# Layer 3 of a fused four-layer forward pass: its distance mask moved into a bias table, its k and v made one group

## What is computed

```python
def odd_layer(x, norm_g, w_in, q_gain, k_gain, sinks, w_out, rel_bias):
    h = rms_norm(x, norm_g) @ w_in                # 2048 -> q 2048, k 256, v 256, gate 2048
    q, k, v, gate = split_cols(h, ODD_SPLITS)
    q = rms_norm(q.reshape(B, T, 32, 64), q_gain)
    k = rms_norm(k.reshape(B, T, 4, 64), k_gain)
    o = swa_sink_attention(q, k, v, sinks, rel_bias)
    return x + (jax.nn.silu(gate) * o) @ w_out

# in swa_sink_attention, W = 128; i a query of a block, j a key of this block or the one before
dist = W + i[:, None] - j[None, :]
bias = rel_bias[t5_bucket(dist)]                  # one number per distance and head
in_window = (dist >= 0) & (dist < W)
logits = jnp.where(mask, logits + bias, -jnp.inf) # then softmax with a sink per head, then times v
```

## Time and profile before

| | |
|---|---|
| median of 3 runs | 1672.68 us (1670.34 to 1673.58) |
| the profiled execution, its own time | 1674.83 us |
| its span | 1672.7 us |
| PE busy | 1524.3 us (91%) |
| PE weight load busy | 1337.2 us (80%) |
| DVE busy | 1085.3 us (65%) |
| ACT busy | 696.4 us (42%) |
| POOL busy | 57.0 us (3%) |
| mean DMA rate | 205 GB/s |
| mean granted clock of TensorE | 0.965 of full |

### The profile page before, as it was taken

The page is one execution under the profiler, slowest core; times in us unless marked ns, Lnnn a source line. Parts: engine busy times, 40 slices in busy tenths (PEclk is TensorE's granted clock), DMA queues, the critical chain, the costliest instruction groups (busy, mean ns, idle before and its releaser), DMA issues.

```text
span 1672.7 us, 25093 instructions
## 1 busy us (share of the span) xinstructions
PE 1524.3 (91%) x9839; PEld 1337.2 (80%) x9839; DVE 1085.3 (65%) x1847; ACT 696.4 (42%) x1186; POOL 57.0 (3%) x86
## 2 busy tenths in 40 slices
PE   5888999988949999999959999999997799989998
PEld 0657789987849888998849998889886798879986
DVE  3436677888977635676675476975646757786563
ACT  1324234334335323444335354544544345655442
POOL 3000000000000000000000000000003300000000
PEclk9898999999979999999979999999999999999999
DMA  9997888997837665775646655326664553334572
GB/s 353 380 380 228 260 273 286 346 348 278 321 130 229 208 181 163 240 259 181 191 138 179 182 147 171 112 76 181 184 185 135 162 165 101 114 114 129 176 220 92
DMA packets 184070, 342.94 MB, mean 205 GB/s; under 512 B 28972, under 2 KB 47632, under 8 KB 183184
## 3 DMA queue, kind: packets, MB, share of 16 engines
q1 hardware_dynamic: 179920, 326.88, 60.7%
q0 software_dynamic: 4032, 14.46, 2.5%
HBM read 339.14 MB, written 2.15 MB: 204 GB/s over the span
## 4 chain that ended last, share of the span: by engine, by line
PE 76%; DVE 9%; DMA 5%; ACT 4%; issue 3%; SPq 2%; POOLq 0%; POOL 0%; DVEq 0%; ACTq 0%
PE PM L1345 63%; PE PB L1345 9%; DMA stg<-in_w_in 3%; SPq L1267 2%; ACT AR L1665 2%; ACT whi L1665 2%; DVE X L1887 1%; PE PB L1517 1%; DVE AC L1887 1%; DVE wlo L1962 1%; PE PB L1489 1%; PE PB L1592 1%; DMA AR<-in_w_in 1%; DMA AR<-in_w_ada 1%; DVE AR L1887 1%
## 5 line engine op out<-in xcount | busy, mean ns | idle before, releaser
L1962 DVE TENSOR_TENSOR wlo<-stg,whi 128x1024 fp32r<-128x1024 f32 (+3 forms) x417 | 492.7, 1190 | 360.7 <-ACT whi L1665 359.8
L1665 ACT ACTIVATE whi<-stg 128x1024 fp32r<-128x1024 f32 (+3 forms) x417 | 425.3, 1025 | 490.4 <-PE PM L1345 382.3
L1345 PE MATMUL PM<-Hh,whi 128*128 128x256 f32 x1824 | 528.8, 293 | 13.4 <-DVE wlo L1962 8.5
L1345 PE MATMUL PM<-Hh,wlo 128*128 128x256 f32 x1780 | 503.1, 286 | 0.0
L1345 PE MATMUL PM<-Hl,whi 128*128 128x256 f32 x1824 | 497.4, 285 | 0.3 <-DVE Hl L2023 0.3
L1345 PEld LDWEIGHTS PM<-Hh,whi 128*128 128x128 f32 x1824 | 354.1, 194 | 34.0 <-issue 15.1
L1345 PEld LDWEIGHTS PM<-Hh,wlo 128*128 128x128 f32 x1780 | 345.8, 194 | 0.0
L1345 PEld LDWEIGHTS PM<-Hl,whi 128*128 128x128 f32 x1824 | 342.6, 193 | 1.3 <-DVE Hl L2023 0.7
L1345 PE MATMUL PM<-whi,Hh 128*128 128x512 f32 (+1 forms) x704 | 276.8, 393 | 9.8 <-DVE Hl L2087 9.8
L1345 PE MATMUL PM<-whi,Hl 128*128 128x512 f32 (+1 forms) x704 | 272.5, 387 | 0.0
L1345 PE MATMUL PM<-wlo,Hh 128*128 128x512 f32 (+1 forms) x704 | 272.4, 387 | 0.0
(11 more groups left out here) (254 smaller groups left out, 1297.3 us busy)
## 6 DMA issues: line engine op xcount, KB each, us to landing
stg<-in_w_ada SPq DMA_DIRECT2D x162, 512.0 KB, 6.4
stg<-in_w_in SPq DMA_DIRECT2D x107, 512.0 KB, 5.3
stg<-in_even_w_in SPq DMA_DIRECT2D x80, 512.0 KB, 3.6
stg<-in_w_out SPq DMA_DIRECT2D x64, 512.0 KB, 4.9
stg<-in_odd_w_in SPq DMA_DIRECT2D x64, 512.0 KB, 3.6
stg<-in_even_w_out SPq DMA_DIRECT2D x32, 512.0 KB, 3.8
stg<-in_odd_w_out SPq DMA_DIRECT2D x32, 512.0 KB, 4.4
AR<-in_w_ada SPq DMA_DIRECT2D x30, 512.0 KB, 11.5
```

The source lines that it names most:

```text
L1345: return e.matmul(out, l, r, start=start, stop=stop, skip_group_check=True)
L1665: return e.activation(out, x, f, **k)
L1962: e.tensor_tensor(wlo[s["slot"]][:, :, 0:n], stg[s["slot"]][:, :, 0:n], whi[s["hi"]][:, :, 0:n].bitcast(F32), ALU.subtract).then_inc(SEM[" ...
```

## The change

- The mask row (384 distances, 0 or -1e30) is loaded into AR in the set-up, added to the table on DVE, and written as a second table of 32 rows to HBM. The constant's semaphore counts 160 in place of 144, the scratch's 32 in place of 16.
- `odd_begin` is gone: its five Toeplitz loads, the load of WM and the 32 additions. In its place `toep_windowed` stands in layer 2's output product, ahead of job 3 of its first group: GT and AC are loaded from the second table, and, once all logits of layer 2 are made, the 16 tiles in AR are loaded again from it. All 32 heads of layer 3 wait for one value.
- k and v are one group of 512 columns, with 24 matmuls in a job, and one step behind it writes both. v leaves PSUM in one ACT instruction in place of two.

```diff
                     if l < 2:
                         self.ln_in = self.tick("ln_landed", 32)
                         self.step("ln_load", l=l, scores=("score_mm", self.count["score_mm"]))
+                    if l == 2:
+                        self.toep = self.tick("toep_landed", 96)
+                        self.step("toep_windowed", logits=("sm_logit", self.count["sm_logit"]), pool=self.pool_mm)
...
-            t_T, t_wm = self.tick("toep_landed", 80), self.tick("wm_landed", 16)
-            self.step("odd_begin", free=tuple(arf), pool=self.pool_mm, T=t_T, wm=t_wm)
             for h in range(32):
-                tm[h] = self.tick("toep_masked")
+                tm[h] = self.toep
...
-        def k_post(pair, mm):
+        def kv_post(pair, mm):
...
-            return [r[-1]]
-
-        self.group([(w, 2048, 256)], [unit("A", 0, n * S, n * 128) for n in range(2)], k_post)
-
-        def v_post(pair, mm):
             Tk["v"] = self.tick("v3_out")
             self.step("v3_out", pair=pair, mm=mm, free=tuple(arf))
-            return [Tk["v"]]
-
-        self.group([(w, 2304, 256)], [unit("B", t, 0, 0, 256, t) for t in range(2)], v_post)
+            return [r[-1], Tk["v"]]
+
+        self.group([(w, 2048, 512)], UKV3, kv_post)
...
+UKV3 = [unit("A", 0, n * S, n * 128) for n in range(2)] + [unit("B", 1, t * S, 256, 256, t) for t in range(2)]
...
+                    (AR[0:32, 0:384], cst[0:32, 4224:4608]), (AR[0:32, 2560:2944], cst[0:32, 3203:3587]), (ONE[:, :], cst[:, 4608:4736])):
...
-                    e.dma_start(scr, AR[0:32, 896:1280]).then_inc(SEM["scr_landed"], 16)
+                    e.dma_start(scr[0:32, :], AR[0:32, 896:1280]).then_inc(SEM["scr_landed"], 16)
+                    q.wait_ge(("buckets", 2))
+                    e.dma_start(scr[32:64, :], AR[0:32, 2560:2944]).then_inc(SEM["scr_landed"], 16)
...
-                elif kind == "odd_begin":
-                    q.wait_all(s["free"])
+                elif kind == "toep_windowed":
                     q.wait_ge(s["pool"])
-                    toeplitz(GT[:, :], 16, 8)
+                    toeplitz(GT[:, :], 48, 8)
                     for n in range(4):
-                        toeplitz(AC[:, n * 512:(n + 1) * 512], 24 + 2 * n, 2)
-                    e.dma_start(ar(WM, 256), cst[:, 3203:3459]).then_inc(SEM["wm_landed"], 16)
-                    for h in range(32):
-                        t = toep("odd", h)
-                        q.wait_ge(s["T"])
-                        q.wait_ge(s["wm"])
-                        e.tensor_tensor(t, t, ar(WM, 256), ALU.add).then_inc(SEM["toep_masked"], 1)
+                        toeplitz(AC[:, n * 512:(n + 1) * 512], 56 + 2 * n, 2)
+                    q.wait_ge(s["logits"])
+                    toeplitz(ar(T0, 4096), 32, 16)
...
-                    for t in range(2):
-                        ins = act(ar(V3 + t * 256, 256), (P0, P1)[t][:, 0:256])
+                    ins = act(ar(V3, 512), P1[:, :])
...
                 e.tensor_copy(AR[0:32, 896:1280], b2[0:32, 0:384]).then_inc(SEM["buckets"], 1)
+                e.tensor_tensor(AR[0:32, 2560:2944], AR[0:32, 2560:2944], b2[0:32, 0:384], ALU.add).then_inc(SEM["buckets"], 1)
```

More of the change, by code:

```diff
@@ L39 @@
 K3, V3, KS3 = 8192, 9216, 11904
-WM = SQ2 + 256
 PT2X = dict(even=(IQ, IQ + 384), odd=(V3 + 512, KS3 + 512))
@@ L1049, in setup @@
             b2, f2 = self.banks.get()
-            self.banks.put(b2, self.tick("buckets"))
+            self.banks.put(b2, self.tick("buckets", 2))
             b3, f3 = self.banks.get()
@@ L1053, in setup @@
             self.step("setup", bank=[b1, b2, b3], free=[f1, f2, f3])
-            self.ar = (("scr_landed", 16), ("rope_tab", 2))
+            self.ar = (("scr_landed", 32), ("rope_tab", 2))
         self.jobs[6]["pre"] = setup_bias
@@ L1188, in build @@
         PM += PB[2:4]
-        scr = nc.dram_tensor("r_scratch", [32, 384], F32, kind="Internal").ap()
+        scr = nc.dram_tensor("r_scratch", [64, 384], F32, kind="Internal").ap()
         cst = A["consts"]
@@ L1243, in upper @@
             return slice(64 * (h % 2), 64 * (h % 2) + 64)
-        const, vec, rope_tab = ("const_landed", 144), ("vec", 1), ("rope_tab", 2)
+        const, vec, rope_tab = ("const_landed", 160), ("vec", 1), ("rope_tab", 2)
         c_in = ("c_landed", 32)
@@ L1268, in sync @@
             q.wait_ge(("out_landed", 128))
-            q.wait_ge(("scr_landed", 16))
+            q.wait_ge(("scr_landed", 32))
         def gpsimd(e):
@@ L1279, in gpsimd @@
                     (CF[:, :, :], cst[:, 1408:1664].rearrange("p (t n) -> p t n", t=2)), (IB[:, :], cst[:, 1664:1667]),
-                    (AR[0:32, 0:384], cst[0:32, 4224:4608]), (ONE[:, :], cst[:, 4608:4736])):
+                    (AR[0:32, 0:384], cst[0:32, 4224:4608]), (AR[0:32, 2560:2944], cst[0:32, 3203:3587]), (ONE[:, :], cst[:, 4608:4736])):
                 e.dma_start(dst, src).then_inc(SEM["const_landed"], 16)
@@ L2351, in constants @@
         c[:, 1667 + 384 * g + 256:1667 + 384 * (g + 1)] = m[128:, 128:]
-    j = np.arange(256)
-    d = p[:, None] + j[None, :] - 127
-    c[:, 3203:3459] = np.where((d >= 0) & (d < 128), 0.0, OFF)
+    d = np.arange(384) - 127
+    c[:, 3203:3587] = np.where((d >= 0) & (d < 128), 0.0, OFF)
     n = np.maximum(np.arange(384) - 127, 0)
```

## The result

| | before | after |
|---|---|---|
| median | 1672.09 us (4 runs, 1670.34 to 1673.58) | 1655.04 us (4 runs, 1652.35 to 1656.47) |
| ratio to before | | 0.9897, 95% interval 0.9879 to 0.9914 |
| profiled execution, its span | 1674.83, 1672.7 us | 1656.47, 1654.4 us |

17.05 us were saved, 1.0%. The forecast was 16.0, and 1656.7 as the new time.

A forecast was written before the change was run, and what follows sets the result against it. PE, busy for 91% of the span, was taken as the bound, with time to regain where it waits or runs at the lower clock. -16.3 + 0.3 = -16.0 us took the median from 1672.68 to 1656.7, range 1652.5 to 1662.5.

The forecast's parts named there:

- The stretch as layer 2's: Layer 3's start takes layer 2's 29.23 us, 32.83 with `k_norm`'s share, in place of 49.12: 16.29 us gained.
- `k_norm` in its new place at 0: In layer 3's q groups `kn_bc`, behind two full jobs, makes PE wait 0 us; bound 1.4 us.
- The mask as part of the same sum, not a term beside it: Removing POOL's 32 additions (27.77 us) adds no separate gain; their cost through DVE is inside the 16.29 us.
- rival 1: Layer 3's start: part of PE's wait only moves; 8.5 us sure, 1664.5 us; chance 0.11.
- The Toeplitz loads at 0: Six loads in layer 2 start at about 1114 us, land by about 1135, and cost 0.
- rival 2: From about 1114 us the weights wait behind the Toeplitz loads; gain 8 us or less, 1665; chance 0.05.
- The set-up at +0.3: One more DVE instruction and two more DMAs in the set-up cost 0.3 us, bounds 0 and 0.9.
- The heads unmoved: Layer 3's heads' steps stay behind the same q jobs; only their clock time moves.
- Rivals 3 and 4: Lower clock in layer 3's q groups, 1721 us, chance 0.03; start's saving given back at the heads, 1672.7 us, chance 0.03.

The follow-up runs named there:

- Experiment 6: The changed kernel with layer 3's three steps between `kn_diag` and `kn_bc` taken away: 1664.67 us, ratio 0.9952 to the kernel before.
- Experiment 2: The changed kernel with k and v as two groups of 256 columns again (mask, table and early loads alone): 1660.49 us, ratio 0.9925 to the kernel before.
- experiment 7: The kernel before with the merged k and v group, POOL's additions waiting until both halves of k are normed: 1661.17 us against 1673.44, ratio 0.9928.
- e1_merge_only: The kernel before with the merged k and v group alone, POOL's 32 additions kept: 1659.76 us against 1672.86, ratio 0.9919.
- e10_warm_all: The changed kernel with useless PE matmuls ahead of the starts of layers 1 to 3 and parts of normed x one job earlier: 1648.55 us, ratio 0.9851.

## Why the prediction was right

Time and range held: 1655.04 in 1652.5 to 1662.5, forecast 1656.7; the gain was 17.05 for 16.0. The mechanism held too: both halves were run apart, and the stretch took the length that was read off layer 2. By its steps:

- *The stretch as layer 2's.* 29.11 us for the 29.23 forecast, and 32.50 for 32.83 with `k_norm`'s share. Against 49.12 before, this is 16.6 us of gain, where the sum had 16.29. The tails say 16.8. Nearly the whole of the gain sits here. That the stretch came within 0.12 us has some luck in it, since layer 2's own stretch differs by 0.54 us between the two profiles. `kn_sum` was put at 0.50 and took 0.34, and the second `kn_swap` took 0.54 where 0.43 was put.
- *`k_norm` in its new place at 0.* Right, with no wait. Experiment 6 prices the cover at 8 to 10 us, so that this 0 had to be argued and not assumed. DVE's part, put at 4.0 us at most, took 3.0 in that experiment.
- *The mask as part of the same sum, not a term beside it.* Right: the merged group alone saves 13.1 us, the mask alone 12.4, both together 17. Whoever adds the two gains forecasts 25.5 us. The 8.5 us that rival 1 called sure was too low for the mask alone (12.4): it counted the 6.7 us wait and 1.8 us of low clock. Experiment 2 shows 5.9 us less in `kn_bc`, 1.9 less for Hh, 1.3 less of the small waits and 2.7 us of PE's busy time. Rival 1 itself falls: no wait of PE is left in the changed stretch.
- *The Toeplitz loads at 0.* Right, also at four times the size, and with them rival 2 falls. They started 1 us ahead of the forecast. The last landed at 1133.6, as said, though it alone took 17.1 us, more than the 12.4 of before. From the first issue this is 20.8 us, between the 12.1 of the sum at 347 GB/s and the 24 of an even share.
- *The set-up at +0.3.* Unresolved: 1.0005 with an interval from 0.9995 to 1.0014 holds both 0 and the term. The DVE part is 0 by its timeline.
- *The heads unmoved.* Right: the same 157 us with the same busy time. Rivals 3 and 4 fall with it and with the clock, which was 1.00 from 1304.68 to 1354 us.

Forecast and median are 1.7 us apart. Of these 0.6 are the kernel before, whose median came out at 1672.09 and not 1672.68, and the other 1.1 are within what executions differ by. Not tried: the changed kernel with its additions on DVE or ACT in place of in the table.

## What to carry to other kernels

Look for a stretch of the same kernel that already has the shape which a change gives to another one: its length, with the moved pieces added, was here better than any sum of single waits. Two edits that act on the same waits don't add up; run each alone before crediting either. Work on POOL that "nobody waits for" can still cost if a chain of small DVE instructions with operands in SBUF runs beside it, and moving it can just pick another chain, as in experiment 7.

## What the hardware showed beyond what was expected

- Beside POOL's additions a DVE instruction of 4 or 16 elements in SBUF took 0.51 to 0.70 us in place of 0.16 to 0.18, and one of 512 or 1024 elements only 0.4 us longer (692 to 1076 ns, 1225 to 1660 ns): a nearly fixed toll per instruction, so that short ones suffer most. It also met a TENSOR_SCALAR with one tile in SBUF as input (L2217, 704 ns, in the changed kernel 168; normed x in e1_merge_only, 954 for 482). Instructions that took nothing more beside POOL: a TENSOR_SCALAR (163 ns, 167 without) and a COPY (420 both times) that read PSUM, and a TENSOR_REDUCE in SBUF (553 ns, 554 without).
- An idle of 5 us on PE was enough for the lower clock in the next 5 us (granted 0.52 from 1276 to 1281), and matmuls of no use in the gap kept it at 1.00. The lower clock also came where the profile shows no idle: for some 3 us in layer 1 (granted 0.50 from 549 to 552 before), within about 1 us of the end of 24 matmuls of one moving column each, in every profile but that of e10_warm_all.
- In layer 2's start the full clock came back at different moments of otherwise like executions: the first 12 transposes and the first job together took 5.9 us in the changed kernel's profile and 6.9 in that of before, with PE at the lower clock up to about 882 and 884 us.
